# TensorE's operands at multiples of 512 bytes, and one subtraction moved ahead of four sums, in a hybrid retention and state-space block with a SwiGLU network

## The reference

```python
D_MODEL = 2048; SEQ = 256; D_FF = 5632
h = rmsnorm(x, norm_mix_g[l])
proj = h @ w_in[l]                       # 2048 x 5120: q, k, v, g, u
...                                      # retention heads; state-space group with w_glu
x = x + mix @ w_out[l]                   # 2048 x 2048
h = rmsnorm(x, norm_ffn_g[l])
x = x + (jax.nn.silu(h @ w_gate[l]) * (h @ w_up[l])) @ w_down[l]
return rmsnorm(x, norm_final_g)
```

## Time and profile before

| | us |
|---|---|
| median of three runs | 1095.27 |
| lowest and highest run | 1095.08, 1095.56 |
| the profiled execution's own time | 1094.16 |
| its span, first to last instruction | 1092.2 |

### The profile page before, as it was taken

One profiled execution on the slowest core, in us unless ns is written; L12 is line 12 of the kernel. 1 busy time (PEld: TensorE's weight loads), 2 busy tenths in 40 slices (PEclk: granted clock), 3 DMA queues, 4 the chain that ended last, 5 costly groups with the idle time before them and its releaser, 6 DMA issues.

```text
span 1092.2 us, 15708 instructions
## 1 busy us (share of the span) xinstructions
PE 1078.0 (99%) x5356; PEld 886.2 (81%) x5356; DVE 977.5 (89%) x1086; ACT 614.0 (56%) x758; POOL 190.4 (17%) x322
## 2 busy tenths in 40 slices
PE   9999999999999999999999999999999999999997
PEld 7878778888988888778888888888888888888876
DVE  7999998754875788999999999999999999999996
ACT  7569544345753566555556455655646465555644
POOL 7130143320100320311030302003030300303010
PEclk9999999999999999999999999999999999999999
DMA  9884588864565667667576665657565765757563
GB/s 361 284 237 144 181 233 244 249 208 150 212 220 186 210 216 228 213 191 221 187 247 202 203 228 187 218 190 242 199 212 193 220 219 176 231 192 234 201 217 120
DMA packets 123802, 232.18 MB, mean 213 GB/s; under 512 B 12016, under 2 KB 19568, under 8 KB 123120
## 3 DMA queue, kind: packets, MB, share of 16 engines
q1 hardware_dynamic: 113392, 215.10, 60.9%
q0 software_dynamic: 9952, 15.62, 5.4%
q10 hardware_dynamic: 416, 0.92, 0.2%
HBM read 218.09 MB, written 5.11 MB: 204 GB/s over the span
## 4 chain that ended last, share of the span: by engine, by line
PE 75%; DVE 16%; issue 4%; DMA 3%; ACT 1%; SPq 0%; DVEq 0%; POOL 0%; POOLq 0%; ACTq 0%
PE ps L1806 33%; PE ps L1770 26%; PE ps L1797 3%; PE ps L1790 3%; PE ps L1794 3%; DVE w_lo L954 3%; DVE w_lo L960 2%; DMA raw<-in_w_in 2%; DVE mix L1356 1%; DVE mix_lo L1342 1%; DVE mix L1350 1%; DVE mix L1348 1%; PE ps L2116 1%; DVE mix L1331 1%; PE ps L2118 1%
## 5 line engine op out<-in xcount | busy, mean ns | idle before, releaser
L564 ACT ACTIVATE w_hi<-raw 128x1024 fp32r<-128x1024 f32 (+1 forms) x166 | 150.0, 927 | 152.5 <-PE ps L1806 80.0
L558 ACT ACTIVATE w_hi<-raw 128x1024 fp32r<-128x1024 f32 x135 | 142.7, 1060 | 153.8 <-DMA raw<-in_w_in 51.7
L954 DVE TENSOR_TENSOR w_lo<-raw,w_hi 128x1024 fp32r<-128x1024 f32 x136 | 163.9, 1220 | 63.2 <-ACT w_hi L558 62.1
L438 POOL DMA_DIRECT2D ff_moved<-ff_turned x184 | 97.0, 535 | 602.4 <-DVE ff_turned L1385 544.1
L960 DVE TENSOR_TENSOR w_lo<-raw,w_hi 128x1024 fp32r<-128x1024 f32 (+1 forms) x166 | 170.0, 1054 | 9.3 <-ACT w_hi L564 9.3
L573 ACT ACTIVATE mix_hi<-mix 128x1024 fp32r<-128x1024 f32 x100 | 104.7, 1057 | 26.9 <-DVE mix L1331 17.0
L1342 DVE TENSOR_TENSOR mix_lo<-mix,mix_hi 128x2048 fp32r<-128x2048 f32 x50 | 114.2, 2284 | 0.0
L564 ACT ACTIVATE w_hi<-raw_more 128x1024 fp32r<-128x1024 f32 x82 | 84.5, 1054 | 48.4 <-PE ps L1770 30.0
L960 DVE TENSOR_TENSOR w_lo<-raw_more,w_hi 128x1024 fp32r<-128x1024 f32 x82 | 97.3, 1216 | 2.1 <-ACT w_hi L564 2.1
L1770 PE MATMUL ps<-w_hi,ffT_hi 128*128 128x512 f32 x320 | 86.9, 394 | 3.1 <-DVE w_lo L960 2.9
L1770 PE MATMUL ps<-w_hi,ffT_lo 128*128 128x512 f32 x320 | 85.7, 390 | 0.0
(11 more groups left out here) (376 smaller groups left out, 2253.4 us busy)
## 6 DMA issues: line engine op xcount, KB each, us to landing
raw<-in_w_in SPq DMA_DIRECT2D x79, 512.0 KB, 5.4
raw<-in_w_gate SPq DMA_DIRECT2D x68, 512.0 KB, 3.8
raw<-in_w_up SPq DMA_DIRECT2D x68, 512.0 KB, 4.6
raw<-in_w_down SPq DMA_DIRECT2D x46, 512.0 KB, 4.3
raw_more<-in_w_down SPq DMA_DIRECT2D x42, 512.0 KB, 3.7
raw<-in_w_out SPq DMA_DIRECT2D x32, 512.0 KB, 3.9
raw_more<-in_w_gate SPq DMA_DIRECT2D x20, 512.0 KB, 4.7
raw_more<-in_w_up SPq DMA_DIRECT2D x20, 512.0 KB, 5.2
```

What stands on the lines that cost most here:

```text
L438: eng.dma_start(moved[32 * b:32 * b + 32, :, a].rearrange("p t k j -> p t (k j)"), turned[32 * a:32 * a + 32, b].rearrange("p t k j -> p t ...
L558: nc.scalar.activation(w_hi[:, n % SPL], raw[:, n % RAW], ACT.Copy).then_inc(S["high_done"], 1)
L564: nc.scalar.activation(w_hi[:, c % SPL, at], raw_of(c)[:, at], ACT.Copy).then_inc(S["high_done"], 1)
L954: tt(w_lo[:, n % SPL], raw[:, n % RAW], w_hi[:, n % SPL].bitcast(F32), ALU.subtract).then_inc(S["low_done"], 1)
```

## The change

Three things are done.

1. A pad of 384 bytes, `to_512`, and the 128x128 identity are put in front of `raw`. As built, `raw` now begins at byte 17408, a multiple of 512, and so do all that were at 128. The overlay that holds sB moves from behind the state-space tables to a place behind the one of `mix_lo`; sB begins at byte 148480, also a multiple of 512. `raw_more`, which only ACT, DVE and DMAs touch, goes from 256 past a multiple of 512 to 64 past one.
2. To make room, `e_tile` (read at the very start) and `bn` (statistics of the heads, written later) share one place, and the pad of 64 bytes goes.
3. In DVE's part of a turn the low part of chunk 18, the third of the `w_down` chunks, stands ahead of the four sums and no longer behind them.

```diff
+        sb("to_512", [P, 96])
+        ident = sb("ident", [P, P])
         raw = sb("raw", [P, RAW, CK])
...
+        m = overlay(
+            [("wbT", [P, 2, BG, P], F32)],
+            [("cl_extra", [P, BG, LOC + 1, CH], F32)],
+            [("dec", [P, 2, SEEN], F32), ("sT", [P, 2, SEEN], F32)],
+            [("sB_hi", [P, 2, 4, P], F32R), ("sB_lo", [P, 2, 4, P], F32R)],
+        )
...
-        sb("to_128", [P, 16])
-        m = overlay(
-            [("wbT", [P, 2, BG, P], F32)],
...
-            [("sB_hi", [P, 2, 4, P], F32R), ("sB_lo", [P, 2, 4, P], F32R)],
-        )
...
-        ident = sb("ident", [P, P])
...
-        e_tile = sb("e_tile", [P, GROUPS])[:]
+        m = overlay([("bn", [P, 2 * HEADS, 6], F32)], [("e_tile", [P, GROUPS], F32)])
+        bn, e_tile = m["bn"], m["e_tile"][:]
...
-        bn = sb("bn", [P, 2 * HEADS, 6])
...
                 loop_low(d, j)
                 ffT_low(j + 1)
                 loop_low(d + 1, j)
+                loop_low(d + 2, j)
                 first_sums(j)
                 last_sums(j)
-                loop_low(d + 2, j)
                 loop_low(d + 3, j)
                 ff(j + 2)
```

More of the change, by code:

```diff
@@ L216, in build @@
         m = overlay(
+            [("wbT", [P, 2, BG, P], F32)],
[3 more added lines that the diff above has]
+        )
+        for part, x in enumerate((m["sB_hi"], m["sB_lo"])):
+            s_mixed[part] += [x[:, i] for i in range(2)]
+        wbT, dec, sT = (m[k] for k in ("wbT", "dec", "sT"))
+        cl_extra = m["cl_extra"][:]
+        m = overlay(
             [("below_cl_room", [P, VEC_COLS], F32), ("cl", [P, CBUF, BG, LOC + 1, CH], F32), ("k_tab", [P, TBUF, BG, P], F32),
@@ L247, in build @@
         qs, qr, rot, zT, sqT, y1T, x_gain = (m[k] for k in ("qs", "qr", "rot", "zT", "sqT", "y1T", "x_gain"))
-        sb("to_128", [P, 16])
-        m = overlay(
-            [("wbT", [P, 2, BG, P], F32)],
-            [("cl_extra", [P, BG, LOC + 1, CH], F32)],
-            [("dec", [P, 2, SEEN], F32), ("sT", [P, 2, SEEN], F32)],
-            [("sB_hi", [P, 2, 4, P], F32R), ("sB_lo", [P, 2, 4, P], F32R)],
-        )
-        for part, x in enumerate((m["sB_hi"], m["sB_lo"])):
-            s_mixed[part] += [x[:, i] for i in range(2)]
         for part in range(2):
             s_mixed[part].append(s_last[part][:])
-        wbT, dec, sT = (m[k] for k in ("wbT", "dec", "sT"))
-        cl_slots = [cl[:, i] for i in range(CBUF)] + [m["cl_extra"][:]]
+        cl_slots = [cl[:, i] for i in range(CBUF)] + [cl_extra]
         m = overlay([("cl_t", [P, BG, LOC + 1, CH], F32), ("kst", [P, 2, 2, KPAD * CH], F32)],
```

## The result

The changed kernel takes 1087.38 us (median of four runs, 1086.34 to 1087.96) against 1095.41 for four runs of the kernel before: a ratio of 0.9924, with a 95% interval of 0.9909 to 0.9939. It is 0.76% faster. The forecast of 1089.3 was 1.9 us too high. It had the sign and the mechanism of the loop; what was gained ahead of the loop it did not have.

A forecast was written before the change was run, and what follows sets the result against it. PE was taken to set the pace, with DVE close behind. Gains of 5.8 (middle turns), 0.1 (first) and 0.1 (last) sum to 6.0 us, so 1095.27 - 6.0 = 1089.3 us, range 1084.5 to 1092.

The forecast's parts named there:

- The loss of 0.82 in a turn: PE's loop turn, 62.70 us against a floor of 61.88: chunk 18 0.41 and 0.13, units 4 and 6 0.24, followers 0.04.
- sB's offset: Units 4 and 6, whose stationary block is sB: its different offset makes matmuls 232 instead of 227 ns, 0.24 us a turn.
- slower: offset 0 is like 256: Rival, all matmuls: even multiples of 256 are slow, 232.4 ns each, a turn of 63.4, 1111 us in all; chance 0.08.
- The rule of 16-byte lines: SBUF reads: 0, 128 and 256 all start a line, none is better; sB's 0.28 us a turn would stay.
- sB stays slow: Rival, units 4 and 6: the slowness has another reason than offset; gain 4.5 us, 1090.8 us in all; chance 0.12.
- Every matmul gets faster: Rival, all matmuls: offset 0 takes away 11 ns each, up to 17 us ahead of the loop, about 1069; chance 0.06.
- DVE takes the gain: Rival, loop: the sums lose 1.13 us each turn, DVE needs 62.29, gain 3.5 us, 1091.8 in all; chance 0.12.
- The new wait for silu: DVE ahead of `ff` in each turn: a new wait of about 0.35 us for ACT's silus.
- The new wait at chunk 22: PE waits about 0.1 us for `down_add(j, 1)`, plus 0.13 to get into step, then not in the next turn.
- the 0.72 a turn: Eight middle turns: gain averaged over two turns, (0.82 + 0.61) / 2 = 0.72 us a turn, 5.8 us in all.
- First and last turn: Loop's ends: a gain of 0.1 us in each, limited by DVE's `down_add` ahead of chunk 22 and chunk 20.
- Ahead of the loop I count nothing: The 433.5 us before the loop: the edits add no instruction and no wait there, so 0 us of gain.

The follow-up runs named there:

- e2: The kernel before with only chunk 18's low part moved ahead of the sums on DVE, all tensors at their old places: 1090.34 us, ratio 0.9961.
- e1: The changed kernel with chunk 18's low part back behind the sums, so only the new places are left: 1090.87 us, ratio 0.9960.
- e6: The changed kernel with `raw`, `w_hi` and `w_lo` back at 128 past a multiple of 512, all else at 0: 1104.63 us, ratio 1.0086.
- e7: The changed kernel with sB alone at a multiple of 512 and all other operands at 128 past one: 1089.89 us, ratio 0.9949.
- e11: The changed kernel itself, unaltered, timed again on the same chip as others: 1087.56 us, ratio 0.9936.
- e8: The changed kernel with `down_add(j, 1)` ahead of chunk 23's low part and, in the last turn, `down_add(j, 0)` ahead of chunk 20's: 1084.88 us.
- e12: The program of e8 again, beside the changed kernel on one chip: 1086.05 us, ratio 0.9920.
- e9: The changed kernel with `raw` alone at 128 past a multiple of 512, TensorE's operands still at 0: 1088.48 us, ratio 0.9942.
- e10: The changed kernel with `raw` alone at 64 past a multiple of 128, TensorE's operands still at 0: 1088.31 us, ratio 0.9942.

## Why the prediction was right, and where it was not

- **The loss of 0.82 in a turn** was accounted for rightly. The wait and the step behind it (0.41 + 0.13) go with the order (e2), units 4 and 6 and their followers (0.28) with the places (e1). Part of it comes back at chunk 22, as forecast.
- **sB's offset** was the right reason, in the form that stood against the rival "slower": a mismatch of two offsets. e6 and e7 show it. Its price of 5 ns a matmul is rounded low: 0.12 over 21 matmuls is 5.7. The rule of 16-byte lines, in the Trainium skill, SBUF — State Buffer, section "Door 1: The DMA port swizzle", cannot tell 0 from 128 and would have left the 4.88; the runs differ from it by 6 ns per matmul in e6, and the measurement decides.
- **"sB stays slow" and "slower: offset 0 is like 256"** fell with the first profile (4.76). **"Every matmul gets faster"** fell too: 226.7 ns at 0, 64, 128 and 256 alike. The 216 ns that the prediction takes from the Trainium skill, TensorE: Matmul & The Clock Gate, section "Back-to-back issue gap", is there the gap of a matmul by itself; for a stream the section gives 131, and the streams here keep 226.7. **"DVE takes the gain"** would have been turns of 62.29; they take 61.96 to 62.05.
- **The new wait for silu** was set at 0.35 and is 0.27.
- **The new wait at chunk 22** had the right sum with the wrong pattern, so that the 0.72 a turn (measured 0.71) is in part luck. I let it cost about 0.2 in every other turn and nothing between; chunk 22 loses 0.08 to 0.14 in each middle turn. In e11, the same program, it does go up and down by turns (0.05 to 0.09, then 0.13 to 0.18), but never to nothing. So "In the next turn PE then has that distance in hand again, and the wait falls away" was wrong: some of it stays in each turn. The step that failed compares the end of the addition with the start of PE's matmul (679.84 and 679.76). What waits is the load of the stationary block, and that begins 0.22 ahead of the matmul, so the cover before was 0.40 us and not 0.62, and e2's 0.54 already uses it up. The middle turns gain 5.65 us in all, 5.8 were forecast. e8 shows that the place is right: with `down_add(j, 1)` one step earlier the loss there is gone.
- **First and last turn** were set at 0.1 each and gained 0.21 and 0.12 in the profiles. Only the last is shown: e11, the same program, took 64.74 in its first turn and lost 0.43 there.
- **"Ahead of the loop I count nothing"** is the step that was wrong, by 1.67 us in the profile, and most of the distance between 1089.3 and 1087.38. I had looked for instructions and waits that the edits add, found none, and not asked whether the pad moves the places where transfers land. Early in the kernel the DMA engines are busy for 0.91 to 0.92, and there they move 339 GB/s instead of 328, while PE waits for `u_tok` no more. Part of the 1.67 belongs to that one execution: the five profiles with the changed places took 425.75 to 426.93 and the two with those of before 426.95 and 427.42, so by their means the places are worth 0.9 us, and the changed program's own stage differed by 0.24 between two profiles, that of e8 and e12, one program, by 0.77. How much of it is `raw`'s (0.75 to 0.9 by the times of e9 and e10, whose ranges overlap with the changed kernel's) and which other tiles have the rest stays open.

## What to carry to other kernels

Let a matmul's stationary block and its stream begin at the same offset in their partitions: with 128 bytes between them a matmul of 512 columns took 233 ns instead of 226.7, and a group that is slower than its neighbour under the same DMA traffic is the sign of it. Before you credit one value of an offset, try the others: here "multiples of 512" did nothing in the loop that 64 or 128 did not do too. And where two engines run within 0.2% of each other, place each instruction that the faster one makes for the slower by its due time, not by habit: two additions moved ahead were worth 1.5 us. And when you ask how much cover a wait has, count to the load of the stationary block and not to the matmul: here that is 0.22 us earlier.

## What the runs showed of the hardware

The penalty of a mismatch is uneven: in e6's down chunks matmuls start in turn 237 to 238 and 229 ns apart, and behind a mismatched group a few matched ones are uneven too, which is why units 5 and 7 took 5.46 and 4.78 instead of 5.44 and 4.76. With equal offsets the pace in the units is 226 to 227 in the changed kernel throughout. At chunk 22 the load of the stationary block begins 0.22 us ahead of its matmul when nothing holds it; where it came only 0.07 ahead, the first four matmuls took 0.97 instead of 0.907. In a stretch where the 16 DMA engines are busy for 0.91 to 0.92, the bytes moved differ by 3% with where the destinations begin, and packets of 4096 bytes take 164 ns in the median instead of 159.
